# Modulation blocks given out four in every second attention unit in place of two in every unit

## The reference, cut to what matters

```
for i in range(DEPTH):                                   # two layers
    m_lat = (silu(c) @ ada_w[i] + ada_b[i])              # ada_w[i]: 1024 x 6144
    m_ctx = silu(c_ctx) @ ada_w[i] + ada_b[i]
    sh1, sc1, g1, sh2, sc2, g2 = split(m_lat, 6)
    h = rms(x, norm1_g[i]) * (1 + sc1) + sh1             # the same for the context rows
    o = mixer(h, hc, ...)                                # layer 0: Fourier mix and window attention
    x = x + g1 * o                                       # layer 1: neighbourhood attention
    h = rms(x, norm2_g[i]) * (1 + sc2) + sh2
    x = x + g2 * swiglu(h, ...)
```

## Time and profile before

| what | us |
| --- | --- |
| median of three executions | 2195.89 |
| span of the profiled execution | 2191.4 |
| TensorE matmuls busy, all of the span | 2102.6 (96%) |
| VectorE busy | 1430.8 (65%) |
| ScalarE busy | 972.3 (44%) |
| GpSimd busy | 315.1 (14%) |
| modulation matmuls (L722), all 96 blocks | 62.0 |
| attention of layer 0, first S to first matmul of the projection | 65.12 |
| attention of layer 1, the same | 72.51 |

### The profile page before, as it was taken

One profiled execution on the slowest core, in us unless ns is written; L12 is line 12 of the kernel. 1 busy time (PEld: TensorE's weight loads), 2 busy tenths in 40 slices (PEclk: granted clock), 3 DMA queues, 4 the chain that ended last, 5 costly groups with the idle time before them and its releaser, 6 DMA issues.

```text
span 2191.4 us, 35302 instructions
## 1 busy us (share of the span) xinstructions
PE 2102.6 (96%) x12873; PEld 1778.8 (81%) x12873; DVE 1430.8 (65%) x2491; ACT 972.3 (44%) x1531; POOL 315.1 (14%) x336
## 2 busy tenths in 40 slices
PE   6999999999989998999999999999999999999998
PEld 2755788888877747999998788999978888888887
DVE  4436544443258585665579767997986677777776
ACT  3335322222244365444475725446743444444444
POOL 0014000000013030000000004787830000000000
PEclk9999999999999999999999999999999999999999
DMA  8266222222335274555644434552246565555553
GB/s 321 85 222 240 87 96 96 96 96 96 97 99 160 82 258 156 170 182 185 209 154 149 166 131 148 164 183 69 68 135 220 180 196 190 190 186 189 191 189 127
DMA packets 92847, 342.90 MB, mean 156 GB/s; under 512 B 10393, under 2 KB 10420, under 8 KB 92224
## 3 DMA queue, kind: packets, MB, share of 16 engines
q1 hardware_dynamic: 89280, 325.10, 44.8%
q0 software_dynamic: 3456, 16.26, 2.4%
HBM read 340.27 MB, written 1.05 MB: 156 GB/s over the span
## 4 chain that ended last, share of the span: by engine, by line
PE 85%; DVE 8%; ACT 3%; issue 2%; DMA 2%; POOL 0%; DVEq 0%; SPq 0%; ACTq 0%; POOLq 0%
PE banks L933 20%; PE banks L1381 16%; PE banks L980 8%; PE banks L1363 7%; PE banks L1275 6%; PE banks L1366 3%; PE banks L1128 3%; PE banks L1324 3%; PE banks L858 2%; PE banks L1308 2%; PE banks L1012 2%; DVE main_zone L1935 2%; PE banks L722 2%; DMA weight_ring<-in_stream 1%; PE banks L884 1%
## 5 line engine op out<-in xcount | busy, mean ns | idle before, releaser
L933 PE MATMUL banks<-act_parts,first_w_parts 128*128 128x512 f32 (+1 forms) x2592 | 476.9, 345 | 7.4 <-DVE act_parts L1938 5.3
L933 PEld LDWEIGHTS banks<-act_parts,first_w_parts 128*128 128x128 f32 x2592 | 410.6, 190 | 70.6 <-issue 8.2
L1938 DVE TENSOR_TENSOR first_w_parts<-weight_ring,first_w_parts 128x1024 fp32r<-128x1024 f32 x166 | 206.9, 1249 | 259.0 <-ACT first_w_parts L1552 259.0
L1381 PE MATMUL banks<-w_parts,a_parts 128*128 128x512 f32 x1536 | 365.7, 392 | 3.9 <-DVE a_parts L1938 3.9
L1381 PEld LDWEIGHTS banks<-w_parts,a_parts 128*128 128x128 f32 x1536 | 290.3, 189 | 63.9 <-issue 4.4
L1938 DVE TENSOR_TENSOR w_parts<-weight_ring,w_parts 128x1024 fp32r<-128x1024 f32 x207 | 253.2, 1223 | 78.1 <-ACT w_parts L1552 78.0
L1552 ACT ACTIVATE w_parts<-weight_ring 128x1024 fp32r<-128x1024 f32 x207 | 218.8, 1057 | 189.2 <-PE banks L1363 102.1
L1552 ACT ACTIVATE first_w_parts<-weight_ring 128x1024 fp32r<-128x1024 f32 x166 | 174.7, 1057 | 232.5 <-PE banks L933 120.6
L1363 PE MATMUL banks<-n_parts,w_parts 128*128 128x512 f32 x632 | 229.4, 397 | 1.3 <-DVE w_parts L1938 1.3
L980 PE MATMUL banks<-ffn_hidden_parts,first_w_parts 128*128 128x512 f32 (+1 forms) x1056 | 183.4, 336 | 0.0
L980 PEld LDWEIGHTS banks<-ffn_hidden_parts,first_w_parts 128*128 128x128 f32 x1056 | 162.6, 190 | 20.5
(11 more groups left out here) (293 smaller groups left out, 3046.5 us busy)
## 6 DMA issues: line engine op xcount, KB each, us to landing
weight_ring<-in_stream SPq DMA_DIRECT2D x618, 512.0 KB, 3.4
main_zone<-in_rel_bias POOLq DMA_DIRECT2D x6, 512.0 KB, 13.1
rounded<-in_dft_input POOLq DMA_DIRECT2D x1, 1600.0 KB, 6.9
main_zone<-in_decay POOLq DMA_DIRECT2D x1, 1536.0 KB, 9.4
rounded<-in_dft_inverse POOLq DMA_DIRECT2D x1, 1280.0 KB, 6.2
main_zone<-in_xT POOLq DMA_DIRECT2D x1, 1024.0 KB, 11.4
main_zone<-in_ctxT POOLq DMA_DIRECT2D x1, 1024.0 KB, 15.9
tail_zone<-in_rel_bias POOLq DMA_DIRECT2D x2, 512.0 KB, 24.5
```

Of the source, the lines that this page charges most:

```text
L933: mm = pe.matmul(o[:, 0:w], wb[:, hw, k, :], fin[:, hx, k, 0:w], start=(k == 0 and n == 0), stop=(k == DC - 1 and n == 2))
L1381: mm = pe.matmul(acc[n][:, :], ap_[:, e % 3, ha, (n // 2) * P:(n // 2 + 1) * P], wp[(B + b) % PARTS][:, hw, (n % 2) * 512:(n % 2 + 1) * 51 ...
L1938: return dve.tensor_tensor(o, a, b, op)
```

## The change

In unit i the kernel before gives out blocks 2i and 2i + 1 of the list. The changed kernel gives out none in an even unit, and in an odd unit the blocks 2(i - 1) to 2i + 1, so four. The blocks and their order are the same, and so is every other instruction. In layer 0, with 30 blocks, unit 15 has two and unit 14 none, where before unit 14 had two and unit 15 none.

```
                 for i in range(PAIRS + 3):
                     if i < PAIRS:
                         scores(i)
-                        for f in fill[l][(1 - l) * EARLY:][i * GROUP:(i + 1) * GROUP]:
-                            ada(*f)
+                        if i % 2:
+                            for f in fill[l][(1 - l) * EARLY:][(i - 1) * GROUP:(i + 1) * GROUP]:
+                                ada(*f)
                     if 0 <= i - 3 < PAIRS:
                         values(i - 3)
                     if 0 <= i - 2 < PAIRS:
                         turn(i - 2)
```

## The result

The changed kernel took 2205.38 us (median of six executions, 2201.26 to 2208.2) against 2196.55 us for the kernel before on the same chip (six, 2194.75 to 2201.26): 8.8 us between the medians. Forecast was 2199.9 us (+4.0), with 2204.5 us as the upper end of the range. The direction of the forecast's sum was right, the size was not.

A forecast was written before the change was run, and what follows sets the result against it. The prediction took TensorE to bound both attentions, with little slack in the VectorE and ScalarE chain. Layer 1 +1.35 and layer 0 +2.6 gave +4.0 us on 2195.89, so 2199.9 us, range 2194.8 to 2204.5.

The forecast's parts named there:

- Start of layer 1: First units of layer 1's attention: without unit 0's free blocks, V of unit 0 comes later, +1.04 us.
- Start of layer 0: First units of layer 0's attention: the last block of unit 3 lands later, +0.4 us (from -0.4 to +1).
- units 4 to 11 of layer 0: Two groups of four units in layer 0: chain 0.70 plus load stall 0.56 us each, +2.5 in all.
- pairs of layer 1: Layer 1, units 4 to 13: five pairs of units, each 0.18 us dearer, +0.9 in all.
- end of layer 1: Last units of layer 1: S of unit 15 comes earlier, so V of unit 13 does too, -0.59 us.
- end of layer 0: Last units of layer 0: unit 14's blocks go into the idle time ahead of V of unit 13, -0.3 us.
- Step 4, the stream: Layer 0 loads go out in bursts of four; the third lands late, stalling units 7 and 11 by 0.56 us each.
- Step 3, the chain of layer 0: Layer 0: ScalarE's copies set V of unit 3 at 9.03 us; four units take 15.18 against 14.48, +0.70.
- Steps 1 and 2: Merged block pairs save 0.13 us; a layer 1 pair of units takes 8.38 against 8.20, 0.18 dearer.
- A: Rival, slower: load bursts meet in layer 0, units 7 and 11 stall 2.7 us each, 2204.2 us; chance 0.17.
- B: Rival, faster: the chain has more slack, neither VectorE nor loads are late, -2.9 us, 2193.0 us; chance 0.10.
- C: Rival, nothing moves: gains and losses cancel, 0 to +2 us, 2197 us; chance 0.18.

The follow-up runs named there:

- e3: Changed kernel plus one 512-column matmul behind S of unit 0 in each attention; ratio 1.0032 [1.0021, 1.0043] to the kernel before.
- e7: Changed kernel with 20 of layer 0's 30 blocks read from resident rows, not loaded; one profile: layer 0 66.60 us, layer 1 76.60.
- e1: Kernel before with the change only from unit 4 on; units 0 to 3 keep two blocks each; ratio 1.0013 [1.0002, 1.0025].
- e2: Kernel before with the change only in units 0 to 3; two blocks per unit from unit 4 on; ratio 1.0029 [1.0019, 1.0038].
- e4: Kernel before with only unit 0's two blocks moved to unit 1; one profile: layer 0 67.54 us, layer 1 75.96.
- e11: Changed kernel itself, unedited, in a second profiled execution: layer 0 71.25 us, layer 1 76.68.
- e8: Kernel before with layer 0's unit 0 pair of blocks moved ahead of its S; one profile: layer 0 62.21 us, layer 1 72.48.
- e5: Changed kernel with the other parity: four blocks in even units, none in odd; ratio 1.0029 [1.0019, 1.0040] to the kernel before.
- e10: Kernel before with layer 0's unit 0 pair of blocks moved ahead of its S, timed in several executions; ratio 0.9996 [0.9986, 1.0006].
- e12: Kernel before itself, unedited, in a second profiled execution: layer 0 64.42 us, layer 1 72.52.

## Why the prediction was wrong, by its own steps

**"Start of layer 1", +1.04, and "Start of layer 0", +0.4: these failed.** They came out at +3.8 and +2.8. The forecast took the two blocks of unit 0 as free work in an idle place, and priced what moves when they leave it at durations from rows with a full clock: S heads of 1.06 us, four blocks of 1.85. Taken out, they left TensorE idle for 0.8 to 1.0 us between two S, and from within the second S on 6.83 us ran at 1.2 GHz. Without the fall the terms themselves were good: 12.65 - 11.68 = +0.97 for layer 1 (e3, whose added matmul stands in the idle place) and 13.80 - 13.17 = +0.63 for layer 0 (e7, whose first units are those of the changed kernel), where two executions of the kernel before differ by 0.4. The fall adds 2.85 in layer 1 (after less e3) and 2.14 in layer 0 (after less e7). Removing the edit from the head removes the fall (e1), the head's edit alone brings it (e2, e4), a matmul in the idle place takes it away (e3). In layer 1 it came in all five profiles that have nothing between the first two S (after, e2, e4, e7, e11) and in none of the nine others. In layer 0 it came in four of those five; the fifth, e7, says that the empty unit makes the fall likely and not certain, and e8 that the gap alone is not enough. What else it takes is open.

The sum, piece by piece: starts +6.6 (forecast 1.44), units 4 to 11 of layer 0 +3.09 (2.5), pairs of layer 1 +1.06 (0.9), end of layer 1 -0.69 (-0.59), end of layer 0 -0.32 (-0.3). Of the 5.7 us that the forecast lacks, 5.1 are in the starts and 5.0 of these are the two falls.

The forecast read the clock in the earlier trace rows, 1.00 in both stretches, and did not use it. The column was a condition on every duration that was taken from there.

In the Trainium skill, "TensorE: Matmul & The Clock Gate" tells under "A second HAM failure mode: psum-queue depth-cycling" of a bf16 kernel whose TensorE idles briefly between groups of matmuls, and so often that its clock goes down and up and it loses throughput. The windows after agree in part: a granted clock of 0.50 behind idle times of 0.81 and 0.98 us, but behind one such place at a start and not behind many. Read beside the empty unit 0, the page would have made a rival of its own.

**Step 4, the stream, 0.56 a stall: too small.** In the first profile unit 7 paid 0.62, unit 11 paid 1.28. The timeline of TensorE in layer 0, S of units 4, 8 and 12, V of unit 3, the A of units 7 and 11, V of unit 13:

```profile
166.22 1.13 PE L884 MATMUL banks<-main_zone 64*128 64x512 f32 x4
...
175.15 0.66 PE L905 MATMUL banks<-tail_zone,main_zone 128*64 128x128 f32 x8 [0.73 <-ACT tail_zone L1542]
...
177.40 2.54 PE L722 MATMUL banks<-weight_ring,small_zone 128*32 128x512 f32 x16
179.86 1.09 PE L905 MATMUL banks<-tail_zone,main_zone 128*64 128x128 f32 x16
...
181.91 1.13 PE L884 MATMUL banks<-main_zone 64*128 64x512 f32 x4
...
193.09 1.91 PE L722 MATMUL banks<-weight_ring,small_zone 128*32 128x512 f32 x12
195.24 1.05 PE L722 MATMUL banks<-weight_ring,small_zone 128*32 128x512 f32 x4 [0.25 <-DMA weight_ring<-in_stream]
...
198.27 1.13 PE L884 MATMUL banks<-main_zone 64*128 64x512 f32 x4
...
213.30 1.09 PE L905 MATMUL banks<-tail_zone,main_zone 128*64 128x128 f32 x16 [0.74 <-ACT tail_zone L1542]
```

Four blocks in 179.86 - 177.40 = 2.46 in place of 1.85 is the stall of unit 7. From unit 4 on the loads are waited for only in those two units, and never in layer 1, as forecast. That 0.62 is so near the forecast is luck of this profile: in e11, the same kernel, four units take 16.15 and 16.02 us, by the same subtraction 1.08 and 0.95, and e3 has 1.40 and 1.33. The prediction's estimate by the Trainium skill's "DMA: Bandwidth & Descriptors" (anatomy of one DMA) had no stall, where the rows have 1.90. But that section's figures are for transfers on the GpSimd path, and these loads go out on the SP queue, so the rows do not speak against the page.

**Step 3, the chain of layer 0: right.** V of unit 3 is 8.93 behind S of unit 4 (forecast 9.03) and four units take 15.07 in e7 (15.18). **Its end: right.** 213.30 - 198.27 = 15.03 (15.0).

**Steps 1 and 2 and the end of layer 1: right.** S of units 4, 6 and 14, the second S of a pair, its blocks, and V of unit 13:

```profile
790.43 1.13 PE L884 MATMUL banks<-main_zone 64*128 64x512 f32 x4
...
798.81 1.13 PE L884 MATMUL banks<-main_zone 64*128 64x512 f32 x4
...
827.41 1.44 PE L884 MATMUL banks<-main_zone 64*128 64x512 f32 x4
828.78 1.92 PE L722 MATMUL banks<-weight_ring,small_zone 128*32 128x512 f32 x16
830.63 1.09 PE L905 MATMUL banks<-tail_zone,main_zone 128*64 128x128 f32 x16
...
832.68 1.13 PE L884 MATMUL banks<-main_zone 64*128 64x512 f32 x4
842.05 1.09 PE L905 MATMUL banks<-tail_zone,main_zone 128*64 128x128 f32 x16 [0.93 <-ACT tail_zone L1542]
```

A pair takes 798.81 - 790.43 = 8.38 (8.38). An odd S takes 828.78 - 827.41 = 1.37, 0.31 more than 1.06 (0.31). Its four blocks take 1.85 (1.85). V of unit 13 is 9.37 behind S of unit 14 (9.47). One of the five pairs took 8.73, since VectorE began 1.58 behind its S and not 1.23; why is open.

**The rivals.** A named about the right time, 2204.2, for a wrong reason, so by luck: the loads cost 1.90 us in units 4 to 11 and not 5.4, and there is no wait in units 5 and 9 or in layer 1. B and C fell with the measurement.

## What to carry to other kernels

Work that fills an idle place of TensorE can be doing two things, its own and keeping the clock up; before it is moved away, price the matmuls behind that place at both levels of the clock, and add the difference to the range. Read the granted clock beside every duration that a sum takes from a trace, and ask whether the edit keeps what the engine did just before. A place ahead of the step on which a last chain starts (S of unit 15 here, in e5) is no place to put work merely because TensorE idles a little later.

## What the runs showed of the hardware that was not expected

- Idle times of TensorE of 0.81 and 0.98 us between two S were followed by a granted clock of 0.50 for 6.83 us; one 512-column matmul put there, 1.05 us, kept it at 1.00 in both places (e3). With a pair of blocks just ahead of the first S, an idle time of 0.84 us was followed by no fall in e8 and by one of 3.4 us in e10.
- The same first units gave a fall in one execution and none in another (layer 0: after and e11 against e7), and the kernel before has a fall near 111 us in one of its two profiles. One profile is not enough to say that a clock holds.
- A stretch that was 2 us shorter in a single profile is not clear of the noise in the timed runs (e10, eleven of them: -0.9 us [-3.1, +1.3]): between two executions of one kernel a head of 13 us moved by 0.4 us (before, e12), and 23 executions of the kernel before beside e5 to e8 lie between 2190.3 and 2201.5 us.
